# Second block's mixers: ScalarE splits the next weights at the head of each place, before it waits for the scaled tile

## The reference

```python
h = rms_norm(x, ln1_g[l]) * (1.0 + sc1) + sh1
z = h @ w_in[l]
u_pool, c_q_raw, c_kv_raw, k_rope_raw, gz_a, gz_b = jnp.split(z, cuts, axis=-1)
y_a = pool_mixer(u_pool, w_pool[l], pool_scale[l]) @ p_pool[l]
y_b = mla(c_q_raw, c_kv_raw, k_rope_raw, ...) @ p_attn[l]
merged = jax.nn.sigmoid(gz_a) * y_a + jax.nn.sigmoid(gz_b) * y_b
x = x + g1 * (merged @ w_out[l])
...
x = x + g2 * (jnp.square(jax.nn.relu(h2 @ w_ff1[l])) @ w_ff2[l])
```

## Time and profile before

| | |
|---|---|
| median of 3 runs | 1988.77 us (1987.45 to 1990.42) |
| the profiled execution | 1989.85 us |
| its span | 1988.5 us |
| granted TensorE clock, mean of the span | 0.988 |
| busy: PE, PEld, DVE, ACT | 96%, 93%, 68%, 53% |

### The profile page before, as it was taken

How to read it: one execution, slowest core, us unless ns; L and a number is a source line. 1 busy time by engine, 2 the same in 40 slices (tenths; PEclk the granted TensorE clock), 3 DMA queues, 4 the chain that set the end, 5 groups by cost and what they waited for, 6 DMA issues and landing times.

```text
span 1988.5 us, 36718 instructions
## 1 busy us (share of the span) xinstructions
PE 1914.6 (96%) x15339; PEld 1857.4 (93%) x15339; DVE 1360.6 (68%) x2417; ACT 1056.6 (53%) x1774; POOL 1.3 (0%) x8
## 2 busy tenths in 40 slices
PE   7999999999999999999999999887999998899998
PEld 7999998899999999989899999877999987899998
DVE  5777665577775777566668776676886557677854
ACT  5444555655444544465666445655665456556643
POOL 0000000000000000000000000000000000000000
PEclk9999999999999999999999999989999999899999
DMA  6776322246784667432346775333455543345553
GB/s 246 261 273 247 128 107 86 107 170 246 262 304 159 233 255 296 170 109 104 113 164 226 288 296 191 122 119 115 174 189 189 189 146 123 127 153 188 191 181 117
DMA packets 51812, 366.07 MB, mean 184 GB/s; under 512 B 6620, under 2 KB 8060, under 8 KB 9792
## 3 DMA queue, kind: packets, MB, share of 16 engines
q1 hardware_dynamic: 51648, 363.72, 50.0%
HBM read 362.65 MB, written 1.05 MB: 183 GB/s over the span
## 4 chain that ended last, share of the span: by engine, by line
PE 82%; DVE 9%; ACT 7%; issue 2%; DMA 1%; SPq 0%; DVEq 0%; ACTq 0%
PE bank L424 23%; PE bank L426 23%; PE bank L425 23%; DVE w_lo L1499 3%; ACT w_hi L1003 3%; PE bank L460 1%; PE bank L456 1%; PE bank L457 1%; DMA raw_a<-in_weights 1%; PE bank L694 1%; PE bank L745 1%; PE bank L744 1%; PE bank L746 1%; PE bank L567 1%; PE bank L622 1%
## 5 line engine op out<-in xcount | busy, mean ns | idle before, releaser
L424 PE MATMUL bank<-xn_hi,w_hi 128*128 128x272 f32 (+2 forms) x2544 | 740.6, 291 | 0.9 <-DVE w_lo L1499 0.9
L426 PE MATMUL bank<-xn_lo,w_hi 128*128 128x272 f32 (+2 forms) x2544 | 729.8, 287 | 0.0
L425 PE MATMUL bank<-xn_hi,w_lo 128*128 128x272 f32 (+2 forms) x2544 | 728.5, 286 | 0.0
L424 PEld LDWEIGHTS bank<-xn_hi,w_hi 128*128 128x128 f32 x2544 | 483.7, 190 | 9.6 <-issue 6.9
L1499 DVE TENSOR_TENSOR w_lo<-raw_b,w_hi 128x1024 fp32r<-128x1024 f32 (+1 forms) x282 | 356.6, 1265 | 196.7 <-ACT w_hi L1003 195.9
L1499 DVE TENSOR_TENSOR w_lo<-raw_a,w_hi 128x1024 fp32r<-128x1024 f32 (+1 forms) x282 | 356.4, 1265 | 188.9 <-ACT w_hi L1003 187.9
L425 PEld LDWEIGHTS bank<-xn_hi,w_lo 128*128 128x128 f32 x2544 | 483.8, 190 | 1.3 <-issue 0.2
L426 PEld LDWEIGHTS bank<-xn_lo,w_hi 128*128 128x128 f32 x2544 | 483.9, 190 | 0.0
L1003 ACT ACTIVATE w_hi<-raw_a 128x1024 fp32r<-128x1024 f32 (+1 forms) x282 | 306.3, 1088 | 230.9 <-PE bank L426 197.6
L1003 ACT ACTIVATE w_hi<-raw_b 128x1024 fp32r<-128x1024 f32 (+1 forms) x282 | 306.6, 1089 | 229.1 <-PE bank L426 215.3
L426 PE MATMUL bank<-h_lo,w_hi 128*128 128x272 f32 (+1 forms) x704 | 201.6, 286 | 0.0
(11 more groups left out here) (324 smaller groups left out, 2924.9 us busy)
## 6 DMA issues: line engine op xcount, KB each, us to landing
raw_a<-in_weights SPq DMA_DIRECT2D x123, 1024.0 KB, 4.6
raw_b<-in_weights SPq DMA_DIRECT2D x123, 1024.0 KB, 4.6
ada_raw<-in_ada_w SPq DMA_DIRECT2D x48, 1024.0 KB, 4.8
raw_a<-in_weights SPq DMA_DIRECT2D x16, 1408.0 KB, 6.1
raw_b<-in_weights SPq DMA_DIRECT2D x16, 1408.0 KB, 5.8
c_rows<-in_c_rows SPq DMA_DIRECT2D x3, 512.0 KB, 3.6
raw_a<-in_weights SPq DMA_DIRECT2D x2, 768.0 KB, 4.3
raw_b<-in_weights SPq DMA_DIRECT2D x2, 768.0 KB, 3.9
```

Source lines behind the costliest of these rows:

```text
L424: pe.matmul(o, wh, xh, start=start, stop=False)
L425: pe.matmul(o, wl, xh, start=False, stop=False)
L426: return pe.matmul(o, wh, xl, start=False, stop=stop)
```

## The change

ScalarE's program of the second block's mixers calls `split_hi(u + 4)` right at the head of places 0 to 38, before anything else. The calls at the end of a place stay; where the unit has been split already they do nothing. In place 13 the count of units is raised before the middle split, not behind it, so that the middle split is that of the second unit. From place 39 on nothing changes, and no other engine's program is touched.

```diff
@@ -1379,6 +1379,8 @@
         u = u0
         for at in range(47):
             finish(chains, at)
+            if at < 39:
+                split_hi(u + 4)
             if at == 9:
                 load_table(EXP_TANH_SET)
             elif at == 41:
@@ -1407,8 +1409,8 @@
             elif at in (12, 13):
                 for part in range(at - 12, 2 * at - 23):
                     if part == 2:
+                        u += 1
                         split_hi(u + 4)
-                        u += 1
                     act.wait_ge(k.sem["unit_done"], u + 1)
                     for h in HEADS_OF[part]:
                         b = QUERY_BANKS[h]
```

## The result

| | before | changed |
|---|---|---|
| median | 1988.39 us (1987.45 to 1990.42, 4 runs) | 1935.47 us (1934.5 to 1937.26, 4 runs) |
| profiled execution's span | 1988.5 us | 1934.2 us |
| mean granted clock | 0.988 | 0.997 |

The ratio is 0.9734, with a 95% interval of 0.9717 to 0.9750: 52.9 us faster by the medians, 54.3 by the two spans. The forecast was 48.5 us faster, 1941.3 us. VectorE's program stands two lines lower in the changed kernel, so L1499 before is L1501 after, L1947 is L1949, and so on.

The account below looks back on a forecast made before the run. TensorE, waiting for the ScalarE-VectorE loop in four second-block mixer stretches, was taken as the bound. 14.4 + 13.9 + 11.7 + 10.2 + 1.7 − 3.4 = 48.5 us off 1989.85 gave 1941.3; range 1929 to 1966, own range 1932 to 1950.

Parts of the forecast that it names:

- What bounds the kernel: Second-block mixers, two stretches per layer: TensorE waits for the ScalarE-VectorE loop; 44.3 us idling plus 18.2 us slow clock, 62.5 us.
- rival (c): Whole span: no change, TensorE's order alone sets the end and waits return elsewhere; 1990 us, chance 0.04.
- First stretch: Places 0 to 16 and the first probabilities' transpose: VectorE stops waiting for shift and split; gains 14.4 and 13.9 us.
- The landing ahead of unit 18's split: Place 13: unit 18's block lands about 1.6 us after ScalarE comes to it, delaying query and key copies.
- Second stretch: First to last probabilities' transpose: low split runs during ScalarE's exponentials, 15.5 us of waiting goes; gains 11.7 and 10.2 us.
- The two middle pairs: Two pairs of places between first and last transpose: VectorE-bound by about 0.6 us each through the pool's high parts.
- my floors: First to last transpose: TensorE's busy time less the clock's loss, 49.8 us in layer 0 and 49.3 in layer 1.
- the pool's wait: First to last transpose: VectorE's 3.5 us wait for the pool's high parts was to stay.
- The shift's lateness: Each scaled tile's shift starts about 0.55 us later; uncovered in all 78 places 43 us, taken as zero.
- Clock: Stalls left in the mixers may bring slow-clock spells; one of 1.7 us charged per layer, 3.4 us.
- (a): Places 19 to 31: ScalarE waits for block landings instead, 24 us of the gain lost; 1965 us, chance 0.16.
- (b): Second-block mixers: all TensorE stalls and slow spells go, 62.5 us gained; 1927 us, chance 0.06.

## Why the prediction was right

**What bounds the kernel.** Right. Cutting the span into four stretches found 62.5 us of idling and slow clock behind a TensorE total of 96%, and the change got 53.8 of them, by the stretches and the way between the layers. The rule of the busiest engine, rival (c), would have said that a ScalarE edit gives nothing.

**First stretch.** Forecast 57.5 and 57.3 us, measured 56.4 in both. VectorE waited 3.3 for high parts, 0.9 and 0.3 for the latents' and 0.8 for TensorE, 5.3 in all where I had 5.7; its work was 49.7 instead of 50.2; and I had rounded 57.2 up. In both layers that is 2.0 us of the difference. That the sum of waits came out so near is in part luck. I had 3.6 us for the ends of units 3, 4 and 5, and they took 0.8; I had 1.4 us for high parts, the first split and place 13, and these two took 0.56 and 0.48, but two more waits that I had at nothing took 0.93 (place 2, while ScalarE was still at the shift of place 1) and 1.34 (the landing in place 4). These are layer 0's; layer 1's waits add up to the same 5.3 in another mix. The landing ahead of unit 18's split was forecast at 1.6 and took 1.45; TensorE's stalls were forecast at 1.3 and took 0.9 ahead of the first scores, 1.0 and 1.3 for the sum of squares, 1 and 0.7 ahead of T0. The runs with the keys first and with the landing behind the copies show that VectorE and not these stalls sets T0, and the run with the sum ahead that removing one is worth nothing.

**Second stretch.** Forecast 51.0 and 50.3, measured 50.6 and 50.6. The two middle pairs were VectorE-bound as said, though not by 0.6 each: against the run with the parts copied first they were 0.3 and 1.4 us longer, together 1.7, where I had 1.2 and 1.0 for the two layers. That the totals agree so well has a second cause: my floors of 49.8 and 49.3 were too high, since without these waits the stretch lasts 49.0. I had let the pool's wait stay at 3.5; it grew to 4.7 in both layers, since the shift ahead of it is late. The 1.7 us are the worth of having these parts ahead of the tile's wait (4.7 to 3.0), so a little more than the lateness alone.

**The shift's lateness.** Taken as zero from bounds of 0 and 43 us. The run with the split behind the shift shows the trade: sparing it costs 24 us. That it is not zero shows in VectorE's waits for the pool's parts (1.2 us more), the latents' (0.8 more) and the attention output's (0.4 more) here, and in the first block's mixers.

**Clock.** I charged one slow spell per layer, 3.4 us; none came, and this term and the first stretch's 2.0 make up 5.4 of the 5.8 us between 48.5 and 54.3. The rest is the 0.5 ahead of the first tile, less 0.1 behind T7. With most of the stall time gone the stretches run at 1.00, where they ran at 0.91 to 0.96. The run of places 15 to 38 and the one with the keys first, which have waits of 3.9 and 3.6 us ahead of T0, pay with slow clock behind them. The Trainium skill, page "TensorE: Matmul & The Clock Gate", section "The HAM clock gate", has the array drop to the lower level after idling; these rows agree in kind.

**Rivals.** (a) did not come: the landings that ScalarE waited for in the first stretch cost it 1.8 and 1.45 us in layer 0, 0.8 and 1.5 in layer 1, and none stands in the second. Of these, the 1.8 us reached VectorE as its wait of 1.34. (b), the ceiling, was nearer than I gave it, 53.8 of 62.5, since VectorE's 50 us of work fits into a stretch of 56.4. The forecast's own range, 1932 to 1950, is narrower than the bounds that I named for it: 11.4 us of waits and 3.4 of clock either way give 1926.5 to 1956.

## What to carry to other kernels

Where two helper engines hand tiles to and fro and each place ends with prefetch work, see which wait of the pair names the other's prefetch: work whose inputs are long there belongs ahead of a wait for something fresh, so that the partner's follow-up never waits for it. Do it only in the stretches where the main engine is held by that pair, found by windows and not by totals; in the one other stage that was tried here, the delayed evacuation was all that came of it, 3.1 us slower. And look afterwards for the one consumer that the partner needs at once, and put it ahead again.

## What was not expected of the hardware

TensorE's clock behind short waits is not regular. Waits up to 1.3 us brought no slow spell in the changed kernel. Ahead of the same transpose, T0, a wait of 1.93 us brought one in one layer and none in the other of the same execution. Longer ones brought one each time, but not of one size: behind 2.70 us in the run of places 0 to 14, T0 to T1 took 2.8 and 1.6 us more than in the changed kernel; behind 3.6 us 1.4 and 1.5 more; behind 3.9 and 3.8 us 1.6 in both layers; behind 4.02 us in the run with the split behind the shift 1.6 and 2.9. In all these runs TensorE waits for nothing between T0 and T1. So a stall of two to four microseconds cost between nothing and about its own length on top of itself, and that decided the size of four experiments here. What sets it in a given layer stays open.
